# One vector instruction for the dilated shift, and a weight split placed behind attention step 11

## What is computed

```python
z = h @ odd_w_in                                  # 1024 -> 3*3*512 + 512
q_c, k_c, v_c = split(z[..., :n_c])               # 3 dilation groups x 8 heads x 64
o_c = _dilated_attention(q_c, k_c, v_c, slopes)
o_d = _multiscale_pool(z[..., n_c:], pool_w, pool_scale)
mixed = concatenate([o_c, o_d], -1) @ odd_w_out   # 1024 -> 1024
x = x + g1 * mixed

# in _dilated_attention, for group g with (window, dil), slopes[g][h] = 2 ** (-8 * (8*g + h + 1) / 24)
s = einsum(q, k) * scale - slopes[g][h] * abs(offs)
s = where(valid, s, MASK_VALUE)                   # then softmax, weights times v, groups combined
```

## Time and profile before

| | |
|---|---|
| median of 3 runs | 857.54 us (856.28 to 860.87) |
| the profiled execution's own time | 856.18 us |
| its span (first to last instruction) | 854.5 us |
| TensorE (PE) busy | 779.9 us, 91% |
| VectorE (DVE) busy | 596.3 us, 70% |
| ScalarE (ACT) busy | 423.7 us, 50% |
| GpSimd (POOL) busy | 64.9 us, 8% |
| mean granted TensorE clock | 0.942 of full |
| DMA | 171.24 MB, mean 200 GB/s |

### The profile page before, as it was taken

The page is one execution under the profiler, slowest core; times in us unless marked ns, Lnnn a source line. Parts: engine busy times, 40 slices in busy tenths (PEclk is TensorE's granted clock), DMA queues, the critical chain, the costliest instruction groups (busy, mean ns, idle before and its releaser), DMA issues.

```text
span 854.5 us, 16791 instructions
## 1 busy us (share of the span) xinstructions
PE 779.9 (91%) x6581; PEld 737.9 (86%) x6581; DVE 596.3 (70%) x856; ACT 423.7 (50%) x665; POOL 64.9 (8%) x72
## 2 busy tenths in 40 slices
PE   3399998985897999999997999999797999999996
PEld 3299986675797999999997999998687999999995
DVE  3976686779857999975447678866446788886444
ACT  4344465331335666665334555545345666666322
POOL 0200116000200000000000004400000000000000
PEclk9799998568899999999999999999898999999998
DMA  9999876321363999855761997665113778865501
GB/s 360 346 265 333 298 264 228 99 75 41 94 195 100 292 291 290 254 196 198 267 224 51 290 340 254 226 199 172 50 50 100 197 221 239 242 222 206 194 2 50
DMA packets 160053, 171.24 MB, mean 200 GB/s; under 512 B 5179, under 2 KB 142340, under 8 KB 158980
## 3 DMA queue, kind: packets, MB, share of 16 engines
q1 hardware_dynamic: 153667, 147.50, 54.6%
q0 software_dynamic: 6336, 23.07, 7.5%
HBM read 169.50 MB, written 1.05 MB: 200 GB/s over the span
## 4 chain that ended last, share of the span: by engine, by line
PE 81%; DVE 12%; DMA 3%; issue 2%; ACT 2%; SPq 1%; DVEq 0%; POOLq 0%; ACTq 0%
PE acc L1130 54%; PE big L1130 14%; DMA ada_raw<-in_ada_w 2%; DVE mod_acc L827 2%; DVE qk L310 2%; PE aux L1190 2%; PE big L1289 1%; PE acc L1294 1%; DVE w_lo L758 1%; PE big L1404 1%; DVE mod_acc L768 1%; DVE work L801 1%; DVE rstd L789 1%; PE aux L1200 1%; DVE o_rms L970 1%
## 5 line engine op out<-in xcount | busy, mean ns | idle before, releaser
L1130 PE MATMUL acc<-h_hi,w_hi 128*128 128x256 f32 x1248 | 353.2, 283 | 17.7 <-DVE h_lo L808 14.8
L1130 PE MATMUL acc<-h_lo,w_hi 128*128 128x256 f32 x1248 | 349.6, 280 | 0.0
L1130 PE MATMUL acc<-h_hi,w_lo 128*128 128x256 f32 x1248 | 349.6, 280 | 0.0
L758 DVE TENSOR_TENSOR w_lo<-w_raw,w_hi 128x1024 fp32r<-128x1024 f32 x220 | 266.6, 1237 | 117.2 <-ACT w_hi L503 117.1
L503 ACT ACTIVATE w_hi<-w_raw 128x1024 fp32r<-128x1024 f32 x220 | 224.6, 1050 | 94.1 <-PE big L1130 62.4
L1130 PEld LDWEIGHTS acc<-h_hi,w_hi 128*128 128x128 f32 x1248 | 239.4, 192 | 20.1 <-issue 18.1
L1130 PEld LDWEIGHTS acc<-h_lo,w_hi 128*128 128x128 f32 x1248 | 238.9, 191 | 0.3
L1130 PEld LDWEIGHTS acc<-h_hi,w_lo 128*128 128x128 f32 x1248 | 238.9, 191 | 0.0
L1130 PE MATMUL big<-hid_hi,w_hi 128*128 (+1 forms) x352 | 97.5, 277 | 0.0
L1130 PE MATMUL big<-hid_lo,w_hi 128*128 (+1 forms) x352 | 97.2, 276 | 0.0
L1130 PE MATMUL big<-hid_hi,w_lo 128*128 (+1 forms) x352 | 97.2, 276 | 0.0
(11 more groups left out here) (193 smaller groups left out, 918.3 us busy)
## 6 DMA issues: line engine op xcount, KB each, us to landing
w_raw<-in_ffn_w_up SPq DMA_DIRECT2D x88, 512.0 KB, 5.0
ada_raw<-in_ada_w POOLq DMA_DIRECT2D x44, 512.0 KB, 5.6
w_raw<-in_ffn_w_down SPq DMA_DIRECT2D x44, 512.0 KB, 4.0
w_raw<-in_odd_w_in SPq DMA_DIRECT2D x40, 512.0 KB, 5.4
w_raw<-in_even_w_in SPq DMA_DIRECT2D x32, 512.0 KB, 6.0
ada_raw<-in_ada_w SPq DMA_DIRECT2D x30, 512.0 KB, 3.9
ada_first<-in_ada_w SPq DMA_DIRECT2D x5, 1024.0 KB, 8.2
w_raw<-in_even_w_out SPq DMA_DIRECT2D x8, 512.0 KB, 5.1
```

Of the source, the lines that this page charges most:

```text
L758: dve.tensor_tensor(w_lo[:, n % SPLIT, part], w_raw[:, n % RAW, part], w_hi[:, n % SPLIT, part].bitcast(F32), ALU.subtract).then_inc(s_lo, 1)
L1130: ins = pe.matmul(dst, lhsT, rhs, start=start and n == 0, stop=stop and n == 2, skip_group_check=True)
```

## The change

The distances in `consts` are multiplied by the group's factor 2 ** (-8 g / 3), so one slope per head serves all 384 columns. `dil_shift` becomes one instruction over 384 columns with an immediate factor, and the 16 slope columns go. On ScalarE and on VectorE the split of unit `OO`+1 moves from the end of unit 19 to a place behind step 11; on ScalarE the rounding to `h_hi[4:8]` moves ahead of step 11.

```diff
@@ constants
-C_SLOPE = C_DIST + TT * ROW
-C_INV = C_SLOPE + 2 * C_HEADS
+C_INV = C_DIST + TT * ROW
...
-        a[:, C_DIST + t * ROW:C_DIST + (t + 1) * ROW] = np.where(ok, off, BIG)
-    for h in range(C_HEADS):
-        a[:, C_SLOPE + 2 * h] = np.where(half, -slope(2, h), -slope(1, h))
-        a[:, C_SLOPE + 2 * h + 1] = np.where(half, -slope(1, h), -slope(2, h))
+        a[:, C_DIST + t * ROW:C_DIST + (t + 1) * ROW] = np.where(ok, off * 2.0 ** (-8.0 * group / C_GROUPS), BIG)
@@ ScalarE, odd_step(p)
-                split_hi(0, n + SPLIT)
+                if p < N_OI - 1:
+                    split_hi(0, n + SPLIT)
@@ ScalarE, after the units
             act.wait_ge(pool_taken, 4)
+            nc.scalar.activation(h_hi[:, 4:8, :], work[:, 4:8, :], ACT.Copy).then_inc(h_hi_ready, 1)
             for s in range(BESIDE_ENDS, STEPS + 4):
                 dilated(s)
                 if s == BESIDE_ENDS:
-                    nc.scalar.activation(h_hi[:, 4:8, :], work[:, 4:8, :], ACT.Copy).then_inc(h_hi_ready, 1)
+                    split_hi(0, OO + 1)
@@ VectorE, dil_shift(s)
-                for at0, at1, k in ((0, T, -slope(0, h)),
-                                    (T, T + 64, consts[:, C_SLOPE + 2 * h:C_SLOPE + 2 * h + 1]),
-                                    (T + 64, ROW, consts[:, C_SLOPE + 2 * h + 1:C_SLOPE + 2 * h + 2])):
-                    col = C_DIST + t * ROW
-                    ins = dve.scalar_tensor_tensor(out=cs[s % 4][:, at0:at1], in0=consts[:, col + at0:col + at1],
-                                                   scalar=k, in1=big[:, s % 2, at0:at1], op0=ALU.mult, op1=ALU.add)
-                return ins
+                col = C_DIST + t * ROW
+                return dve.scalar_tensor_tensor(out=cs[s % 4], in0=consts[:, col:col + ROW], scalar=-slope(0, h),
+                                                in1=big[:, s % 2, 0:ROW], op0=ALU.mult, op1=ALU.add)
@@ VectorE, the units of the odd projection and after
-                if p >= FIRST_HEADS:
+                if FIRST_HEADS <= p < N_OI - 1:
                     split_lo(0, OI + p + SPLIT)
             for s in range(BESIDE_ENDS, STEPS + 3):
                 dilated(s)
                 if s == BESIDE_ENDS:
                     mixed_lo(MIX_AT[1] + 1, slice(4, 8))
+                    split_lo(0, OO + 1)
```

## The result

The changed kernel takes 872.44 us (median of 4, 871.5 to 873.39), the kernel before 859.2 (median of 4, 856.28 to 867.22). The ratio of the runs is 1.0135, 95% interval 1.0086 to 1.0184 (the two medians alone give 1.0154). The forecast was 849.8 with 0.03 for slower, and it was wrong in sign. Yet the stretch that it worked out came nearly as written. Both things have to be read from the trace.

What follows compares the result with a forecast made beforehand. TensorE was taken as the bound, idle then half-clocked at the hole after unit 19. Savings 4.75 + 2.68 + 0.25 = 7.7 us from 856.18 gave 848.5; the median's 1.36 more made it 849.8, range 847.0 to 853.0.

Steps and rivals of the forecast that it cites:

- The smaller constants load: Constants tile: loading 16 columns less and moving addresses by 64 bytes cost nothing, being beside the first layer's work.
- The rival for "slower": Second 24 matmuls after step 13: the moved split becomes their last wait, over 0.5% slower, from 615.9 us; chance 0.03.
- The idle time, 4.75: Hole on PE after unit 19: the first 24 matmuls start at 598.82 instead of 603.57, saving 4.75 us.
- The clock, 2.68: First 24 matmuls behind the hole: at full clock they take 2.73 us instead of 5.41, saving 2.68.
- The one-instruction shift, 0.55 and 0.25 on the path: DVE's shift: one instruction takes 0.55 us against 0.80 for three; 0.25 counts in the tail, at block 15.
- Step 13 just in time: PE's step 13: `ctok` of block 9 reaches PE at 602.78, due at 602.87, with 0.1 us to spare.
- The clock's fall at later holes, 0.75 either way: Later holes such as norms ahead of up projections: the clock may fall at another moment, allowed 0.75 us either way.
- The total without the address: Whole kernel: forecast 849.8 us, with the 64-byte address move counted as nothing; chance 0.67.

Runs made afterwards that it cites:

- e15: Changed kernel with 64 bytes directly ahead of `h_hi`, so `h_hi`, `h_lo` and the tiles behind them return to their addresses of before; 847.31 us.
- e3: The changed kernel again, unaltered, on the chip of the padded and address-moved kernels; 870.76 us (median of 4), ratio 1.0124 to the kernel before.
- e1: Changed kernel with 16 unused columns ending the constants tile, restoring the addresses of before; 851.22 us (median of 10), ratio 0.9905 to the kernel before.
- e2: Kernel before with its slope columns in a tile behind all others, giving the changed kernel's addresses; 879.7 us (median of 4), ratio 1.0224.
- e14: The kernel before, unaltered, profiled in a second execution; 857.68 us.
- e4: Kernel before with the moved split and rounding alone, three shift instructions, addresses of before; 855.99 us (median of 10), ratio 0.9942.
- e8: Kernel before with the one-instruction shift alone, old order, padded to keep all addresses; 857.3 us (one run).
- e17: Changed kernel with weights 64 bytes higher and activations 128 bytes higher; 850.79 us (median of 4), ratio 0.9887 to the kernel before.
- e9: Changed kernel with 48 unused columns of constants, tiles behind them 192 bytes above the changed kernel's; 863.35 us.
- e11: Changed kernel with all activations (`h_hi`, `h_lo`, hidden tiles) 32 bytes higher and nothing else moved; 869.88 us.
- e7: Changed kernel with 64 bytes between `h_lo` and the hidden tiles, moving only the hidden tiles and buffers behind `h`; 870.77 us.
- e5: Changed kernel with 32 unused columns of constants, tiles behind them 128 bytes above the changed kernel's; 880.8 us.

## Why the prediction was wrong, point by point

**What failed.** One clause: "The smaller constants load (16 columns less) and the addresses moved by 64 bytes: nothing, their load is beside the first layer's work." The load was indeed nothing (e15 has the smaller load and the lowest time). The addresses were put at nothing without asking what their move does to the matmuls, and they were 24.1 us in the profiled executions (16.9 of span lost, and 7.2 won in the tail). As medians on one chip: e3 against e1 some 20 us, e2 against the kernel before 21.0. All 5280 such matmuls (110 units of 48) at 5.3 ns each would make 28.0; the kernel before runs some of them at 117.8 (e14), and ahead of 264 part of the loss fell into waits (PE is busy 7.0 longer there, the window is 2.4 longer). No other term of the sum had all of these matmuls behind it. A change that removes bytes from a tile moves every tile behind it, and that belongs among the things moved. The rival for "slower" (the split becomes the last wait) was the wrong mechanism: its `w_lo` was ready at 617.2, three microseconds before the second 24 matmuls started.

**The idle time, 4.75:** right. Start of the first 24 matmuls 4.73 after unit 19 in the changed kernel, 4.73 in e1 and 4.72 in e4.

**The clock, 2.68:** right in kind. The granted clock was 1.00 over the whole tail. The size was off by 0.3: the first 24 matmuls take 3.02 in e1 and e4, not 2.73. In e1 they follow each other at 117 to 118 ns, the second pace, while the second 24 do at 113; that is 0.1 of it. The other 0.2 was there at equal pace too (3.04 and 2.85 in the changed kernel): the first 24 follow products with the values, the second 24 a transpose, and the 2.73 was read from the second. With 4.68 for the idle time (9.41 to 4.73), 2.39 for the clock (5.41 to 3.02) and 0.25 for the shift, 7.7 became 7.3.

**The one-instruction shift, 0.55 and 0.25 on the path:** both right (0.549 mean, tail of e8 0.25 shorter). The Trainium skill, "Vector Engine (DVE) Microarchitecture Reference", section 5.2, would have had 0.15 for the two instructions taken away; three took 0.80 and one takes 0.55, so here it was 0.25.

**Step 13 just in time:** the working held. Unit 19 ended 15.99 later in this trace, so `ctok` of block 9 was forecast to end at 618.64; it ended at 618.67, and PE had no idle time for it. That 0.1 us to spare became over 0.4 is luck: the first 24 matmuls took 0.3 longer, so the values started later.

**The clock's fall at later holes, 0.75 either way:** with the addresses of before, the second layer's up window took 122.80 in e1 against 122.39, and 121.45 in e15; inside what was allowed. At the hole itself the clock's cost varied too: 4.81 (e14), 5.41 and 5.46 (e8) for the same 24 matmuls.

**The total without the address:** 851.22 for e1, with 849.8 forecast; it would have been in the range. That base varies as well: the kernel before has medians from 857.5 to 862.1 in the different sets of runs, so the ratio (0.9905, forecast 849.8 / 857.54 = 0.991) says more. The Trainium skill, "SBUF — State Buffer", section "Operand start alignment", says what places are allowed for an operand and that those runs "timed nothing"; all layouts here keep its rule, being multiples of 4 bytes, and they differ by up to 6% in pace.

## What to carry to other kernels

When an edit changes the size of a tile, compare the pace of the untouched matmuls (one long row of the chain) before reading anything else; if it moved, pad the tile and measure again, or the verdict on the edit is a verdict on its addresses. Here the edit by itself is worth 0.9% and its 64 bytes cost 2.2% to 2.3% (e2 against before, e3 against e1); with 16 unused columns (e1, median of 10), or the padding directly ahead of `h_hi` (e15, one run), it beats both kernels. Place tiles that feed TensorE together at addresses that you choose, and keep them fixed, instead of letting them follow whatever lies ahead.

## What the runs showed of the hardware

- The pace of float32r matmuls (128x128 by 256 columns, weights and data from SBUF, clock at its 2.4 GHz level) goes by the distance modulo 256 bytes between the tiles with the weights and those with the data: in the down stages 113.4 ns at 192, 117.8 at 64, 118.7 at 128, 118.7 or 120.0 at 160, 120.0 at 0. Each of the four values came on at least two of the three chips of the experiments.
- A stretch can run at another pace with the layout and the granted clock unchanged: 117.8 instead of 113.4 at 192 (e4's second layer, e17's first, the odd projection in e14), 113.4 instead of 117.8 at 64 (e9 from 80 to 95), 120.0 instead of 118.7 at 160 (e11), and at 128 in the up stages of e7. A stage in the second pace of 192 costs some 2 us down (50.88 against 48.96) and 4 us up (126.68 against 122.66). The runs of one kernel scatter by 7 to 12 us (848.58 to 859.12 in e4, 868.69 to 875.77 in e3, 855.49 to 867.8 for the kernel before beside e1), and part of that may be this; how much isn't shown.
- The difference between 113.4 and 118.7 stays where no DMA runs and DVE and ACT do equal work (91 against 87 matmuls in 10 us, in the section on the result).
- The 48 float32 matmuls of `mod_sum` (line 1196 of the changed kernel), both operands ahead of the moved tiles, took 5.35 us in every layout. The 16 float32 matmuls of the norm behind the first down stage, with operands on both sides, took 3.72 us at 192 (before), 128 (changed) and 0 (e5).
